# Three whole up blocks instead of five, another order at two places of the out product, and a weight sum moved from a transfer to VectorE, in a transformer block on one Trainium2 core

## The chip, the cores and the metric

One core of a Trainium2 chip. The time is the device time of one execution in microseconds (us), as the median of several runs. The engines are TensorE (PE in the profile), VectorE (DVE), ScalarE (ACT), GpSimd (POOL) and SyncE (SP, which only issues DMAs here). Every engine works through its own list of instructions in order; semaphores hold an instruction back until another engine or a transfer has counted far enough. A change below 0.2% (5.5 us) can't be told from none here.

## What is computed

One block with 512 tokens and a width of 2048, in fp32: a modulation from a vector `c`, attention over a sliding window beside a gated linear recurrence, an out product, and a feed-forward part with a short convolution.

```python
mod = jax.nn.silu(c) @ w_mod[l] + b_mod[l]
sh1, sc1, g1, sh2, sc2, g2 = jnp.split(mod[:, None, :], N_MOD, axis=-1)
...
merged = jax.nn.sigmoid(gate_a) * y_a + jax.nn.sigmoid(gate_b) * y_b
x = x + g1 * rms_norm(merged @ w_out[l], post_mix_norm[l])
h = rms_norm(x, pre_ffn_norm[l]) * (1.0 + sc2) + sh2
y = conv_ffn(h, w_ffn_up[l], ffn_conv_w[l], ffn_conv_b[l], w_ffn_down[l])
x = x + g2 * rms_norm(y, post_ffn_norm[l])
```

`conv_ffn` is `u = h @ w_up`, its halves `a` and `b` (5504 columns each), a causal convolution of three taps on `a`, `gelu(a) * b`, and the product with `w_down`.

## The kernel before

**fp32 by three products.** Each operand is split into a high half (the value rounded to the type that TensorE multiplies in one pass) and a low half (the rest). ScalarE casts the high half (`split_hi`), VectorE subtracts it (`split_lo`), and TensorE adds hi x hi, lo x hi and hi x lo (`three`). A piece of weights is 128x1024 (512 KB), loaded into a ring of four raw buffers by SyncE's queue and split into two buffer pairs.

**The stages** in order: the start with the modulation, the heads, the pairs (gates and branch products, giving `merged`), the out product (pieces P3 to P3+31, two row blocks of 128 each, four column groups of 512), the norms and the transposition of `h2`, the up product (43 blocks of 128 columns of `a` and of `b`), the down product, the last norm. Between the pairs and the out product `merged` is split as well, row block by row block, into `m_hi` (ScalarE) and `m_lo` (VectorE). In the out product VectorE also adds up `g2` from 64 pieces of 256 KB that GpSimd's queue loads (`g2_half`, L2036), two per piece; the last five pieces are kept and multiplied row group by row group, so that the norms can start. After the product of a row group, VectorE and ScalarE form the norm, GpSimd stores the row group, and VectorE then scales it in place.

**Whole and cut blocks.** The first WHOLE = 5 blocks of the up product are multiplied plainly: four pieces of 24 matmuls over 512 tokens, 96 matmuls. The other CUT = 38 blocks are 2x2 products (two halves of the rows of `h2`, a and b columns of the weights, two halves of the tokens), done with seven products instead of eight, from sums of weights and sums of halves of `h2`. A piece of a cut block is 8 matmuls over [hi | lo] and 8 over the high half alone. The four raw pieces of a block are X11, X21, X12, X22; even blocks have them in `raw`, odd ones in `raw_odd`. The weight sums are X21 + X22 (`w_sums[:, 0]`), that plus X11 (`w_sums[:, 1]`), X12 plus the latter, and X11 + X21. Of these, X21 + X22 is made by a second load of X21 into `w_sums` (`cut_load_s1`) and an adding transfer of GpSimd's queue (`s1_sum`), X11 + X21 by an adding transfer (`s3_sum`), the others by VectorE (`w_sum`). Before each adding transfer GpSimd runs a tiny instruction for order (`pool_turn`, L2417). The sums of halves of `h2` (`half_step`, `half_hi`, `half_lo`) are made by VectorE and ScalarE during the whole blocks. `raw_odd` shares memory with them, so the loads of the second cut block wait for the last of them.

The order of everything is written out by hand in each engine's function; there is no scheduler.

## Time and profile before

| | us |
|---|---|
| median of 3 runs (2767.45 to 2768.26) | 2767.5 |
| the profiled execution | 2769.19 |
| its span, first to last instruction | 2767.7 |
| TensorE busy | 2690.7 (97%) |
| VectorE busy | 1813.0 (66%) |
| ScalarE busy | 1077.1 (39%) |
| GpSimd busy | 231.2 (8%) |

The mean granted clock of TensorE is 0.99 of full speed. A row of a timeline gives the start from the beginning of the span, the duration, the engine, the line, the operation with output<-input, the number of instructions merged into the row, and in brackets how long the engine had stood idle and what released it. Instructions overlap at their ends: matmuls of 512 columns last 0.39 us each and start 0.227 apart, so work is counted from start to start.

### The profile page before, as it was taken

The numbers are of one execution on the slowest core, as the hardware profiler recorded it, in microseconds if no ns is written. First come the engines' busy times: TensorE is split into PE (matmuls) and PEld (weight loads), VectorE is DVE, ScalarE is ACT, GpSimd is POOL, SyncE is SP. The second block draws the span as 40 slices with busy tenths as digits, with TensorE's granted clock in tenths as the row PEclk, the third lists the DMA queues.
The fourth block names the chain that finished last, engine by engine and source line by source line (L and its number), as shares of the span: only waits on it lengthen the run. The fifth ranks groups of instructions, "written<-read, shape, count | busy, mean of one in ns | idle before, by whom it ended". The sixth has DMA issues, their size and how long they took to land.

```text
span 2767.7 us, 41356 instructions
## 1 busy us (share of the span) xinstructions
PE 2690.7 (97%) x14334; PEld 2258.3 (82%) x14334; DVE 1813.0 (66%) x2746; ACT 1077.1 (39%) x1466; POOL 231.2 (8%) x342
## 2 busy tenths in 40 slices
PE   5999999999999999999989999999999999999998
PEld 4788888888788888878778788888888888888886
DVE  6856666666665665545676688888888883334334
ACT  4354444445522222232243344444444442223223
POOL 0030000000000000002200122221212110000000
PEclk8999999999999999999999999999999999999999
DMA  9942232322377777646733888878787856522222
GB/s 361 325 111 84 84 85 84 85 84 80 92 214 219 219 214 219 190 135 209 249 122 115 197 205 198 207 192 211 193 212 191 211 145 221 203 99 96 95 99 106
DMA packets 504710, 460.91 MB, mean 167 GB/s; under 512 B 23419, under 2 KB 418962, under 8 KB 501920
## 3 DMA queue, kind: packets, MB, share of 16 engines
q1 hardware_dynamic: 469584, 360.75, 44.2%
q0 software_dynamic: 25120, 94.54, 12.9%
q10 hardware_dynamic: 9904, 4.26, 0.6%
q8 instruction: 64, 1.05, 0.2%
q14 instruction: 38, 0.31, 0.0%
HBM read 398.66 MB, written 20.99 MB: 152 GB/s over the span
## 4 chain that ended last, share of the span: by engine, by line
PE 92%; DVE 3%; DMA 2%; ACT 1%; issue 1%; SPq 1%; DVEq 0%; POOL 0%; POOLq 0%; ACTq 0%
PE acc_bank L650 15%; PE acc_bank L652 15%; PE acc_bank L651 15%; PE acc_bank L1071 7%; PE acc_bank L1075 3%; PE bank_ta L1071 3%; PE bank_tb L1071 2%; PE bank_pb L1071 2%; PE two_banks L1071 2%; PE two_banks L650 2%; PE two_banks L651 2%; PE two_banks L652 2%; PE bank_ta L1075 1%; PE bank_pb L650 1%; PE bank_pb L1075 1%; PE bank_tb L1075 1%
## 5 line engine op out<-in xcount | busy, mean ns | idle before, releaser
L626 DVE TENSOR_TENSOR w_lo<-raw,w_hi 128x1024 fp32r<-128x1024 f32 x305 | 373.3, 1224 | 692.5 <-ACT w_hi L620 692.5
L620 ACT CAST w_hi<-raw 128x1024 fp32r<-128x1024 f32 x305 | 320.2, 1050 | 884.9 <-PE acc_bank L652 422.4
L650 PE MATMUL acc_bank<-h_hi,w_hi 128*128 128x512 f32 x1124 | 447.3, 398 | 6.4 <-DVE h_lo L1670 6.4
L652 PE MATMUL acc_bank<-h_hi,w_lo 128*128 128x512 f32 x1124 | 439.1, 391 | 0.0
L651 PE MATMUL acc_bank<-h_lo,w_hi 128*128 128x512 f32 x1124 | 438.7, 390 | 0.0
L650 PEld LDWEIGHTS acc_bank<-h_hi,w_hi 128*128 128x128 f32 x1124 | 211.6, 188 | 50.4 <-issue 6.5
L652 PEld LDWEIGHTS acc_bank<-h_hi,w_lo 128*128 128x128 f32 x1124 | 211.5, 188 | 45.3
L651 PEld LDWEIGHTS acc_bank<-h_lo,w_hi 128*128 128x128 f32 x1124 | 211.8, 188 | 41.9
L1071 PE MATMUL acc_bank<-h_pair,s_hi 128*128 128x512 f32 x608 | 152.2, 392 | 0.0
L1656 DVE SCALAR_TENSOR_TENSOR acc<-raw,csil,acc 128x512 f32<-128x512 f32 x180 | 135.1, 750 | 10.1 <-DMA raw<-in_w_mod_dram 5.6
L1071 PEld LDWEIGHTS acc_bank<-h_pair,s_hi 128*128 128x128 f32 x608 | 109.4, 189 | 19.5
L650 PE MATMUL acc_bank<-o_hi,w_hi 128*128 128x512 f32 x256 | 101.0, 394 | 0.6 <-DVE o_lo L1981 0.3
L652 PE MATMUL acc_bank<-o_hi,w_lo 128*128 128x512 f32 x256 | 99.7, 390 | 0.0
L651 PE MATMUL acc_bank<-o_lo,w_hi 128*128 128x512 f32 x256 | 99.6, 389 | 0.0
L650 PE MATMUL acc_bank<-w_hi,a_hi 128*128 128x512 f32 x246 | 95.7, 389 | 0.0
L651 PE MATMUL acc_bank<-w_lo,a_hi 128*128 128x512 f32 x246 | 95.7, 389 | 0.0
L652 PE MATMUL acc_bank<-w_hi,a_lo 128*128 128x512 f32 x246 | 95.7, 389 | 0.0
L2417 POOL TENSOR_TENSOR st<-ones 128x1 f32<-128x1 f32 x76 | 65.6, 864 | 310.2 <-DMA raw<-in_w_ffn_up_dram 141.1
L2147 DVE TENSOR_TENSOR w_lo<-raw,w_hi 128x1024 fp32r<-128x1024 f32 x57 | 69.6, 1221 | 33.3 <-ACT w_hi L1488 33.3
L1488 ACT CAST w_hi<-sums 128x1024 fp32r<-128x1024 f32 x38 | 40.0, 1052 | 130.7 <-DMA sums<-raw_odd 66.0
L2147 DVE TENSOR_TENSOR w_lo<-raw_odd,w_hi 128x1024 fp32r<-128x1024 f32 x57 | 69.6, 1220 | 30.4 <-ACT w_hi L1488 30.4
L2386 POOL DMA_DIRECT2D gain_scratch<-small x1 | 0.6, 554 | 1046.8 <-ACT small L1405 1046.8
(556 smaller groups left out, 5887.5 us busy)
## 6 DMA issues: line engine op xcount, KB each, us to landing
raw<-in_w_in_dram SPq DMA_DIRECT2D x148, 512.0 KB, 4.0
raw<-in_w_mod_dram SPq DMA_DIRECT2D x96, 512.0 KB, 4.5
raw<-in_w_ffn_up_dram SPq DMA_DIRECT2D x96, 512.0 KB, 7.0
raw<-in_w_ffn_down_dram SPq DMA_DIRECT2D x86, 512.0 KB, 3.6
raw_odd<-in_w_ffn_up_dram SPq DMA_DIRECT2D x76, 512.0 KB, 7.5
sums<-in_w_ffn_up_dram SPq DMA_DIRECT2D x38, 512.0 KB, 4.5
mods_low<-in_w_mod_dram SPq DMA_DIRECT2D x32, 512.0 KB, 9.4
raw<-in_w_out_dram SPq DMA_DIRECT2D x32, 512.0 KB, 4.2
```

The lines of the kernel that those rows point to most:

```text
L620: act.copy(w_pair(g, gp)[0][:], raw[n % RAW][:]).then_inc(hi_ready, 1)
L626: dve.tensor_tensor(w_l[:], raw[n % RAW][:], w_h[:].bitcast(F32), ALU.subtract).then_inc(lo_ready, 1)
L650: pe.matmul(o, stat[0], mov[0], start=start, stop=False)
L651: pe.matmul(o, stat[0], mov[1], start=False, stop=False)
L652: return pe.matmul(o, stat[1], mov[0], start=False, stop=stop)
L1071: pe.matmul(CUT_FULL[p], wh[:, k, :], mov[:, k, :], start=k == 0, stop=False)
L1075: pe.matmul(CUT_BANKS[p], wl[:, k, :], mov[:, k, 0:H], start=False, stop=False)
L1488: act.copy(S_HI[S_PAIR[p]][:], cut_source(s, p)).then_inc(hi_ready, 1)
L1656: return STT(dst, w, cs, dst, ALU.mult, ALU.add).then_inc(mod_ops, 1)
L2147: TTe(S_LO[S_PAIR[p]][:], cut_source(s, p), S_HI[S_PAIR[p]][:].bitcast(F32), ALU.subtract).then_inc(lo_ready, 1)
L2386: pool.dma_start(g_scr[0:KT], small[0:KT, 0, 0:P]).then_inc(grow_stored, 16)
L2417: pool.tensor_tensor(st[:, 1:2], ones[:, 0:1], ones[:, 0:1], ALU.add).then_inc(pool_order, 1)
```

## The change

- WHOLE is 3 and CUT is 40.
- X21 + X22 is made by VectorE (`w_sum(s, it, 1)`), right before the first split of that block; the second load of X21 and its adding transfer go. `s3_sum` waits for VectorE's sum, since it overwrites X21.
- The halves of `h2` that the sums start from are kept by ScalarE during the transposition (`keep_y`, 16 copies), in place of three sums of high and low halves by VectorE afterwards; the remaining half steps stand in the two looped whole blocks.
- At the start of the out product VectorE's column operations and first weight split stand before the last product of the pairs, its last merge after two low halves of `merged`, and the third weight split after fourteen; TensorE starts with the eight matmuls of row block 0 that need only high halves.
- The 64 g2 additions go by `g2_done`: one or two per piece at first, then three, all done by piece 25, where they were two per piece to the end.

```diff
-WHOLE = 5
+WHOLE = 3
...
-            def cut_load_s1(s, it):
-
-                sp.dma_start(w_sums[:, 0, :].rearrange("p (k n) -> p k n", k=8), cut_cols(s, it, 0, 1)).then_inc(s1_landed, 16)
-
...
+                        if g == P3 and k == 0:
+                            pe.wait_ge(mh_ready, 1)
+                            for t4 in range(TT):
+                                for part in (wh, wl):
+                                    pe.matmul(OUT_BANKS[bank_set][t4], m_hi[:, 0, t4 * P:(t4 + 1) * P], part[:, 0, :],
+                                              start=part is wh, stop=False)
+                            pe.wait_ge(m_split, 1)
+                            for t4 in range(TT):
+                                pe.matmul(OUT_BANKS[bank_set][t4], m_lo[:, 0, t4 * P:(t4 + 1) * P], wh[:, 0, :], start=False, stop=False)
+                            continue
...
+            def keep_y(kb):
+
+                act.wait_ge(h2x, kb + 1)
+                if kb < 8:
+                    act.copy(RO[8]["y_top"][:, :, kb, :], small[:, kb % 4, :].rearrange("p (h t) -> p h t", h=2)).then_inc(hh_ready, 1)
+                else:
+                    act.copy(y_raw[22][:, kb - 8, :], small[:, kb % 4, H:T]).then_inc(hh_ready, 1)
...
-            weighed(3, KT // 2 - 1)
-            merge(1, KT // 2 - 1)
-
             dve.wait_ge(mod_taken, SUMS_LAST)
...
             split_lo(dve, P3, N3)
+            weighed(3, KT // 2 - 1)
             for kb in range(KT):
                 if kb == 2:
+                    merge(1, KT // 2 - 1)
                     split_lo(dve, P3 + 1, N3 + 1)
+                if kb == 14:
+                    split_lo(dve, P3 + 2, N3 + 2)
...
-            for i in range(2, 34):
-                if i < 32:
-                    split_lo(dve, P3 + i, N3 + i)
-                if i == 2:
-                    dve.wait_ge(multiplied, P3)
-                for half in range(2):
-                    g2_half(2 * (i - 2) + half)
+            def g2_done(i):
+                return min(max(0, i - 3, 3 * i - 12), 4 * KT)
+
+            dve.wait_ge(multiplied, P3)
+            for i in range(3, 32):
+                split_lo(dve, P3 + i, N3 + i)
+                for j in range(g2_done(i), g2_done(i + 1)):
+                    g2_half(j)
...
-                if n == 2:
-                    dve.wait_ge(s1_ready, 16 * (s + 1) + it * 32)
+                if n == 1:
+                    cut_landed(dve, s, it, X21)
+                    cut_landed(dve, s, it, X22)
+                    TTe(w_sums[:, 0, :], cut_raw(s, X21), cut_raw(s, X22), ALU.add).then_inc(s1_ready, 1)
+                elif n == 2:
+                    dve.wait_ge(s1_ready, s + 1 + it * 2)
...
                 else:
+                    w_sum(s + 1, it, 1)
                     cut_lo(s + 1, it, 0)
...
-            def s1_sum(s, it=0):
-
-                pool.wait_ge(s1_landed, 16 * (s + 1) + it * 32)
-                cut_landed(pool, s, it, X22)
-                pool_turn(2 * s + 1, it)
-                pool.dma_start(w_sums[:, 0, :], cut_raw(s, X22), accum_op=ALU.add).then_inc(s1_ready, 16)
...
                 cut_landed(pool, s, it, X21)
-                pool_turn(2 * s, it)
+                pool.wait_ge(s1_ready, s + 1 + it * 2)
+                pool_turn(s, it)
```

VectorE's list at the start of the out product, before the change. `small` and `merged` are the last products and merges of the pairs, `w_lo` the weight splits, `m_lo` the low halves of `merged`:

```order
L1987 TENSOR_TENSOR small<-small,acc_bank 128x512
L1991 TENSOR_TENSOR merged<-small 128x512
L2002 SCALAR_TENSOR_TENSOR a<-modc,vec 128x16
L2003 TENSOR_TENSOR gcol<-modc,vec 128x16
L626 TENSOR_TENSOR w_lo<-raw,w_hi 128x1024
L2010 TENSOR_TENSOR m_lo<-merged,m_hi 128x512 x2
L626 TENSOR_TENSOR w_lo<-raw,w_hi 128x1024
L2010 TENSOR_TENSOR m_lo<-merged,m_hi 128x512 x14
L626 TENSOR_TENSOR w_lo<-raw,w_hi 128x1024
```

The same place after the change:

```order
L2014 SCALAR_TENSOR_TENSOR a<-modc,vec 128x16
L2015 TENSOR_TENSOR gcol<-modc,vec 128x16
L616 TENSOR_TENSOR w_lo<-raw,w_hi 128x1024
L2002 TENSOR_TENSOR small<-small,acc_bank 128x512
L2025 TENSOR_TENSOR m_lo<-merged,m_hi 128x512 x2
L2006 TENSOR_TENSOR merged<-small 128x512
L616 TENSOR_TENSOR w_lo<-raw,w_hi 128x1024
L2025 TENSOR_TENSOR m_lo<-merged,m_hi 128x512 x12
L616 TENSOR_TENSOR w_lo<-raw,w_hi 128x1024
```

The column operations and the first weight split moved ahead of the last product, the merge behind two low halves, and the third weight split ahead of the last two.

VectorE's list at the change from one cut block to the next, in the second block, before the change. `sums` are the weight sums, `s_lo` and `w_lo` splits, `small` and `acc` sums of results:

```order
L2147 TENSOR_TENSOR s_lo<-raw_odd,s_hi 128x1024
L2147 TENSOR_TENSOR w_lo<-raw,w_hi 128x1024
L2182 TENSOR_TENSOR small<-acc_bank,small 128x256
L2154 TENSOR_TENSOR sums<-sums,raw 128x1024
L2172 TENSOR_TENSOR small<-acc_bank,small 128x256
L2147 TENSOR_TENSOR w_lo<-sums,w_hi 128x1024
```

The same place after the change:

```order
L2162 TENSOR_TENSOR s_lo<-raw_odd,s_hi 128x1024
L2170 TENSOR_TENSOR sums<-raw 128x1024
L2162 TENSOR_TENSOR w_lo<-raw,w_hi 128x1024
L2201 TENSOR_TENSOR small<-acc_bank,small 128x256
L2173 TENSOR_TENSOR sums<-sums,raw 128x1024
L2191 TENSOR_TENSOR small<-acc_bank,small 128x256
L2162 TENSOR_TENSOR w_lo<-sums,w_hi 128x1024
```

One row is new, the sum from two raw pieces (L2170); the others keep their order.

## Rows read from the trace of the kernel before

**Rows 1.** The page: the chain that ended last, by engine

```profile
PE 92%; DVE 3%; DMA 2%; ACT 1%; issue 1%; SPq 1%; DVEq 0%; POOL 0%; POOLq 0%; ACTq 0%
```

**Rows 2.** Busy us of PE, PEld, DVE, ACT, POOL in a stretch; clock, DMA

```profile
1640.00:1740.00 100.00, 100.00 (x573) 87.93 (x573) 87.76 (x135) 46.82 (x56) 21.77 (x27) 1.00 0.83 203
```

**Rows 3.** TensorE's timeline, two stages: start us, us, instruction, count [idle before <-releaser]

```profile
1499.87 0.39 PE L650 MATMUL acc_bank<-h_pair,w_hi 128*128 128x512 f32 x1
...
1500.55 0.39 PE L650 MATMUL acc_bank<-h_pair,w_hi 128*128 128x512 f32 x1
...
1916.35 2.00 PE L1071 MATMUL two_banks<-h_pair,w_hi 128*128 128x512 f32 x8
...
1935.91 2.00 PE L1071 MATMUL two_banks<-h_pair,w_hi 128*128 128x512 f32 x8
```

**Rows 4.** TensorE's timeline, the first two cut blocks

```profile
1535.23 1.98 PE L1071 MATMUL two_banks<-h_pair,w_hi 128*128 128x512 f32 x8
...
1542.19 1.10 PE L1075 MATMUL bank_ta<-t,w_lo 128*128 128x256 f32 x7 [1.41 <-DVE w_lo L2147]
...
1564.35 3.78 PE L1071 MATMUL bank_ta<-t,w_hi 128*128 128x512 f32 x8 [4.18 <-ACT w_hi L1488]
...
1572.78 2.00 PE L1071 MATMUL bank_pb<-h_pair,w_hi 128*128 128x512 f32 x8
```

**Rows 5.** ScalarE's timeline in the second cut block

```profile
1563.25 1.05 ACT L1488 CAST w_hi<-sums 128x1024 fp32r<-128x1024 f32 x1 [12.47 <-DMA sums<-raw_odd]
```

**Rows 6.** GpSimd's timeline in the second cut block

```profile
1553.51 0.86 POOL L2424 DMA_DIRECT2D sums<-raw_odd  x1
```

**Rows 7.** TensorE's timeline at the start of the out product

```profile
1221.48 0.47 PE L650 MATMUL acc_bank<-w_hi,m_hi 128*128 128x512 f32 x1 [1.55 <-DVE m_lo L2010]
...
1225.89 0.40 PE L650 MATMUL acc_bank<-w_hi,m_hi 128*128 128x512 f32 x1
```

**Rows 8.** VectorE's timeline at the start of the out product

```profile
1218.01 0.69 DVE L1987 TENSOR_TENSOR small<-small,acc_bank 128x512 f32<-128x512 f32 x1 [4.03 <-PE acc_bank L652]
...
1219.51 1.22 DVE L626 TENSOR_TENSOR w_lo<-raw,w_hi 128x1024 fp32r<-128x1024 f32 x1
1220.65 1.28 DVE L2010 TENSOR_TENSOR m_lo<-merged,m_hi 128x512 fp32r<-128x512 f32 x2
```

**Rows 9.** ScalarE's timeline at the start of the out product

```profile
1220.05 7.38 ACT L1403 CAST m_hi<-merged 128x512 fp32r<-128x512 f32 x14
```

**Rows 10.** TensorE's timeline in the last column group of the out product

```profile
1376.17 0.50 PE L650 MATMUL two_banks<-out_hi,m_hi 128*128 128x512 f32 x1 [1.70 <-DVE out_lo L626]
...
1379.40 0.50 PE L650 MATMUL two_banks<-w_hi,m_hi 128*128 128x512 f32 x1 [1.56 <-DVE w_lo L626]
```

**Rows 11.** VectorE's timeline in the last column group

```profile
1373.37 1.61 DVE L2036 SCALAR_TENSOR_TENSOR x_again<-y,csil,x_again 128x512 f32<-128x512 f32 x2 [0.61 <-DMA y<-in_w_mod_dram]
...
1376.61 1.60 DVE L2036 SCALAR_TENSOR_TENSOR x_again<-y,csil,x_again 128x512 f32<-128x512 f32 x2 [0.49 <-DMA y<-in_w_mod_dram]
1378.13 1.22 DVE L626 TENSOR_TENSOR w_lo<-raw,w_hi 128x1024 fp32r<-128x1024 f32 x1
```

**Rows 12.** VectorE's timeline after the out product

```profile
1401.01 1.28 DVE L2070 TENSOR_SCALAR y<-y,st 128x2048 f32<-128x2048 f32 x1 [3.16 <-DMA x_scratch<-y]
```

**Rows 13.** VectorE's timeline in a cut block of the loop

```profile
1928.73 1.22 DVE L2147 TENSOR_TENSOR s_lo<-raw_odd,s_hi 128x1024 fp32r<-128x1024 f32 x1
...
1940.34 1.23 DVE L2147 TENSOR_TENSOR w_lo<-raw,w_hi 128x1024 fp32r<-128x1024 f32 x1 [1.75 <-ACT w_hi L1488]
```

**Rows 14.** Adding transfers into the sums: count, KB each, median us to landing

```profile
sums<-raw POOLq DMA_DIRECT2D x19, 512.0 KB, 7.0
```

**Rows 15.** ScalarE's timeline in the same block

```profile
1941.69 1.05 ACT L1488 CAST w_hi<-raw 128x1024 fp32r<-128x1024 f32 x1 [0.86 <-PE bank_ta L1076]
```

**Rows 16.** GpSimd's timeline: one instruction, early and in the loop

```profile
1532.78 0.18 POOL L2417 TENSOR_TENSOR st<-ones 128x1 f32<-128x1 f32 x1 [11.45 <-DMA sums<-in_w_ffn_up_dram]
...
1923.93 0.99 POOL L2417 TENSOR_TENSOR st<-ones 128x1 f32<-128x1 f32 x1
```

More of the change, by code:

```diff
@@ L177, in block_kernel @@
             [(f"t{n}", [P, 8, T], F32R) for n in (1, 2, 3)]
-            + [(f"y{n}", [P, 8, H], F32) for n in (21, 11, 12, 22)],
+            + [("y21", [P, 8, H], F32), ("y_top", [P, 2, 8, H], F32), ("y22", [P, 8, H], F32)],
             [("t_home", [P, 6, 8, H], F32R), ("raw_odd", [P, 4, PIECE], F32), ("sums", [P, 2, PIECE], F32),
@@ L200, in block_kernel @@
         end_hi, end_lo, end_ah, end_al = (RO[10][n] for n in ("end_hi", "end_lo", "end_ah", "end_al"))
-        y_raw = {n: RO[8][f"y{n}"] for n in (11, 12, 21, 22)}
+        y_raw = {11: RO[8]["y_top"][:, 0], 12: RO[8]["y_top"][:, 1], 21: RO[8]["y21"][:], 22: RO[8]["y22"][:]}
         raw_odd, w_sums, gelu_out = RO[9]["raw_odd"], RO[9]["sums"], RO[9]["gelu_out"]
@@ L297, in block_kernel @@
         t_step = sem("t_step")
-        s1_landed, s1_ready, s3_ready = sem("s1_landed"), sem("s1_ready"), [sem(f"s3_ready{i}") for i in range(2)]
+        s1_ready, s3_ready = sem("s1_ready"), [sem(f"s3_ready{i}") for i in range(2)]
         sums_ready, mid_out, halves = sem("sums_ready"), sem("mid_out"), sem("halves")
@@ L1410, in square_out @@
                    accum_out=ssg[:, 4 * cg + t4:4 * cg + t4 + 1]).then_inc(y1_sq, 1)
-            for i in range(2, 32):
+            for i in range(3, 32):
                 split_hi(act, P3 + i, N3 + i)
@@ L1441, in _ @@
                     act.wait_ge(h2_ready, kb - 3)
+                    act.wait_ge(hh_ready, KT + kb - 3)
                 A_(small[:, kb % 4, :], TURN6[kb % 6], ACT.Identity, scale=a1[:, 1, kb:kb + 1],
                    bias=modc[:, MOD_SH2 + kb:MOD_SH2 + kb + 1]).then_inc(h2x, 1)
+                if kb >= 2:
+                    keep_y(kb - 2)
                 if kb == 5:
@@ L1446, in _ @@
                     split_hi(act, P4 + 3, N4 + 3)
+            for kb in range(KT - 2, KT):
+                keep_y(kb)
             def half_hi(n, dst):
-                act.wait_ge(t_step, 4 + n)
-                act.copy(dst, y_raw[(11, 12, 22, 21)[n - 1]][:]).then_inc(hh_ready, 1)
+                act.wait_ge(t_step, (3, 2, 4, 5)[n - 1])
+                act.copy(dst, y_raw[(12, 11, 22, 21)[n - 1]]).then_inc(hh_ready, 1)
             def gelu(it):
+                if it == 1:
+                    act.wait_ge(hh_ready, 2 * KT)
                 act.wait_ge(conv_step, it * 3)
@@ L1465, in _ @@
                         act.copy(acc[0:KT, 0:P], SC1[0:KT, 0:P]).then_inc(grow_ready, 1)
-                    if it == 3 and k < 3:
-                        half_hi(k + 1, RO[8][("t1", "t3", "t2")[k]][:, :, 0:H])
+                    if it == 2 and k < 3:
+                        half_hi(k + 1, RO[8][("t3", "t1", "t2")[k]][:, :, 0:H])
             def cut_hi(s, it, p):
@@ L1475, in cut_hi @@
                     if p == 1:
[L1476 removed]
+                        act.wait_ge(s1_ready, s + 1 + it * 2)
                     elif p == 4:
@@ L2016, in conv @@
                 dve.wait_ge(gelu_ready, it)
+                if isinstance(it, int) and it == 0:
+                    dve.wait_ge(hh_ready, 2 * KT)
                 TS(cv, a[:], j(tap_c[2]), j(convb_c), ALU.mult, ALU.add).then_inc(conv_step, 1)
@@ L2036, in g2_half @@
                 return STT(dst, g2_in[j % 4], csil[:, kt:kt + 1], dst, ALU.mult, ALU.add).then_inc(mod_ops, 1)
-            for i in range(2, 34):
-                if i < 32:
-                    split_lo(dve, P3 + i, N3 + i)
-                if i == 2:
-                    dve.wait_ge(multiplied, P3)
-                for half in range(2):
-                    g2_half(2 * (i - 2) + half)
+            def g2_done(i):
+                return min(max(0, i - 3, 3 * i - 12), 4 * KT)
+            dve.wait_ge(multiplied, P3)
+            for i in range(3, 32):
+                split_lo(dve, P3 + i, N3 + i)
+                for j in range(g2_done(i), g2_done(i + 1)):
+                    g2_half(j)
                 if i in (9, 17, 25):
@@ L2136, in _ @@
                         dve.wait_ge(multiplied, P4 + 4)
-                    if it < 3:
+                    if it == 1 or k == 0:
                         half_step(4 * (it - 1) + k)
-                    if it == 3 and k < 3:
-                        n = (1, 3, 2)[k]
-                        half_lo(k + 1, RO[8][f"t{n}"][:, :, 0:H], RO[8][f"t{n}"][:, :, H:T])
+                    else:
+                        n = (3, 1, 2)[k - 1]
+                        half_lo(k, RO[8][f"t{n}"][:, :, 0:H], RO[8][f"t{n}"][:, :, H:T])
             def cut_lo(s, it, p):
```

43 lines of the change are left out of this document (15 added, 28 removed).

## The prediction

> **What bounds the kernel now.** I read the page first, then the waits of TensorE in order of time, then the neighbours of each wait. The chain that ended last is 92% TensorE [rows 1]: only TensorE's own work and its pauses count. In the loop of cut blocks it is busy for 100 us out of 100 at full clock, VectorE for 87.8 [rows 2]. So the reader should look for TensorE work that goes, and for pauses outside that loop.
>
> The work: in a whole block three matmuls start within 0.68 us (1499.87 to 1500.55), and it has 96, so 21.76 us; a cut block takes 1935.91 - 1916.35 = 19.56 us, seven pieces of 2.794 us [rows 3].
>
> The pauses that the change touches are three. At the entry of the cut blocks, ten pieces take from 1535.23 to 1572.78, 37.55 us, where they need 10 x 2.794 = 27.94: 9.6 us are lost [rows 4]. In the second block TensorE stands 4.18 us, and the eight matmuls behind it then take 3.78 us where the same eight take 2.00 (the lower of its two clock levels, 1.2 for 2.4 GHz). What it waits for is ScalarE's cast of the sum X21 + X22, and that one had stood 12.47 us for the adding transfer [rows 5], issued at 1553.51 and landed at 1563.25, 9.7 us later [rows 6].
>
> At the start of the out product, the matmuls run from 1221.48, and the thirteenth starts at 1225.89 [rows 7]. The last piece before it ends at 1218.0: VectorE's product that waits for it starts at 1218.01 [rows 8]. From 1218.0 to 1225.9 TensorE does work worth 12 x 0.2267 = 2.7 us in 7.9: 5.2 us lost, of which 1.7 to the lower clock (1225.89 - 1221.48 = 4.4 us for 2.7 of work). VectorE has its merge, two column operations and a split of 1.22 us (from 1219.51) before the first low half, at 1220.65 [rows 8]. In the last column group TensorE pauses 1.70 and 1.56 us for a split [rows 10]; VectorE does that split late (1378.13) because it does g2 additions first, and stands 0.61 and 0.49 us in them for their own loads [rows 11].
>
> **The change part by part.** *Two whole blocks become cut ones.* 2 x (21.76 - 19.56) = 4.4 us off TensorE's path. The two also bring 2 blocks of VectorE work, which lies beside TensorE.
>
> *The sum X21 + X22 by VectorE.* A load of 512 KB and an adding transfer go; VectorE gets one addition of 128x1024 before its first split of the next block. The trace has the same form at 1.23 us (the split at 1940.34 reads two such operands and writes one [rows 13]), 1.14 from start to start. At the entry: the raw pieces of the first cut block are loaded during the last whole block, so VectorE can add them right after that block's last split, convolution and half matrix, before TensorE is done with it; the cast follows when its buffer is free, about 1535.3 (one matmul group past 1535.23), and TensorE wants it at 1535.23 + 2.79 = 1538.0. For the second block the four loads start when the last half matrix is split (estimate 1537.5), and the addition stands after the last split of the first block (estimate 1550, from the same place in the loop: 1928.73 is 7.2 us before 1935.91, and the second block would start at 1554.8). TensorE wants its cast at 1535.23 + 8 x 2.794 = 1557.6. Nothing of the 9.6 us is left by this count. I take all 9.6. The ends are 4 (rival one) and 9.6; below nothing is excluded, since the transfer that TensorE waited for 4.18 us isn't there any more.
>
> In the loop VectorE goes from 87.8% to (0.878 x 19.56 + 1.14) / 19.56 = 94%. The addition pushes what is queued behind it by 1.14 us: the next block's first two splits, the second sum, and the output sums. VectorE stands 1.75 us before the fourth split, waiting for ScalarE [rows 13], and takes it up there. Cost 0. If that cover were gone, it would cost 1.14 us a block at most, 46 us over 40 blocks, and only once the lead was used up that VectorE has here: it starts these splits 7.2 us before TensorE starts the block (1928.73 to 1935.91).
>
> A wait is added: GpSimd's other adding transfer (X21 += X11) overwrites X21, so it now comes after VectorE's addition, at about 1931.1 in the block shown, plus GpSimd's small ordering instruction, about 1.0 (its row is below), plus 7.0 from issue to landing [rows 14]: 1939.1. ScalarE casts it at 1941.69 [rows 15], and TensorE needs the cast at 1935.91 + 4 x 2.794 = 1947.1, so the data by 1946.0: 2.6 us ahead of ScalarE, 6.9 ahead of TensorE. Behind the transfer in GpSimd's queue stands only the store of an activation, whose slot is used again two blocks later. Cost 0, bounded by the 9.7 us of rows 6 as well, where 4.2 us of lead are left.
>
> GpSimd's small instruction takes 0.18 us early and 0.99 in the loop, where VectorE is busy [rows 16]. The Trainium skill (SBUF — State Buffer, "SBUF: two separate sides") says that a VectorE operation with two SBUF inputs and a GpSimd operation that reads SBUF exclude each other for a whole instruction. The trace agrees so far as these two rows go. By that rule the added operation can hold GpSimd up by one more such instruction, 1.2 us per block, and the transfer lands at 1940.3 instead of 1939.1: the sum stays, and rival four would decide 1.2 us earlier, for which I would give it 0.06 in place of the chance below.
>
> *The start of the out product.* The weight split stands before the last product of the pair stage, and TensorE's first eight matmuls need only the high half: they can start when that product is done, 1218.01 + 0.69 = 1218.7. The pause falls to 0.75 us and I take the clock as kept. The third weight split now stands behind 14 low halves: start of the first 1218.63, two, the merge, a split, twelve more at 0.61 each, so it ends at 1230.1, and TensorE wants it at 1218.75 + 96/2 x 0.2267 = 1229.6. That costs 0.45. ScalarE is no later: its casts are 0.53 us apart (7.38 for 14 [rows 9]). Gain 5.2 - 1.2 = 4.0; with the clock lost again 2.3.
>
> *The g2 additions* are done by piece 25, three per piece from the fifth. Then nothing stands between the last splits, and the pauses of 1.70 and 1.56 go: 3.3 us. What is late next is the last piece's own load, which the split frees one addition earlier than before. In pieces 5 to 25 VectorE does three additions of 0.8 (two take 1.61 [rows 11]) and a split of 1.14 in the 24 x 0.2267 = 5.44 us of a piece, beside TensorE. Everything after the out product starts 3.3 us earlier, but VectorE waits there 3.16 us for a store that GpSimd issues only after TensorE's g2 sum [rows 12]; that sum moves with TensorE, so I count the 3.3 once.
>
> *ScalarE's 16 copies in the turn of h2* (0.5 us each) lie in its waits for TensorE; they replace VectorE's first three sums of halves. Cost 0: TensorE gets its h2 rows several steps ahead. Of the half steps that were spread over three whole blocks, eight now stand in two, one to a piece; at 1.22 us for 1024 columns I estimate 2.4 for 2048, and with the split 3.6 of the 5.44 us of a piece. At the last piece the convolution comes on top (three passes, some 2.2), once, with the lead of a split behind it.
>
> Sum: 4.4 + 9.6 + 4.0 + 3.3 = 21.3 us. The profiled execution takes 2769.19 us (span 2767.7 and 1.5 around it), so 2747.9; the median of the runs, 2767.5, is 1.7 below it, so **2746.2 us**.
>
> **The rivals.** *One: the second cut block still stands.* The second adding transfer of that block now waits for VectorE's addition, about 1551.6, and is issued at 1552.5 in the busiest stretch of DMA; with the 9.7 us of rows 6 it lands at 1562.3, with its cast 1563.4, where TensorE wants it at 1535.23 + 11 x 2.794 = 1566.0. Only 2.6 us stand between. If it fails, a pause and the slow clock behind it come back, as in rows 4: about 5.5 of the 9.6 us, so 2751.7.
>
> *Two: the g2 loads hold VectorE.* When VectorE took them as fast as they came, two additions went in 1376.61 - 1373.37 = 3.24 us, 1.62 each [rows 11]; three need 4.9 of 5.44. A 1 MB load on the same queue comes in three times. Should each addition take 2.0, three and a split no longer fit, VectorE falls behind by up to 0.6 us a piece for 20 pieces, and after some 4 us of lead TensorE waits for up to 8: 2754.
>
> *Three: more comes.* VectorE no longer adds after the last piece, so its first row product starts sooner; if the 3.16 us of rows 12 go too, 2743.0. Against it: the store is behind the same TensorE sum.
>
> *Four, the other side: the adding transfer is late in every block.* If VectorE's addition and GpSimd's order bring it past 1946.0, TensorE waits in every one of 40 blocks. It decides when issue to landing passes 7.0 + 6.9 = 13.9 us, and the kernel is slower than before by over 0.2% from 27 us / 40 = 0.67 us per block, 14.6. At 1 us per block: 2746.2 + 40 = 2786. Against it: 9.7 is the longest seen in these rows, and a load and a transfer per block are gone from the DMA queues.
>
> **How the numbers follow.** Forecast 0.61, rival one 0.12, two 0.09, three 0.13, four 0.04; 0.01 is left for no effect. The range takes in one, two and three: 2742 to 2754. A difference below 0.2% (5.5 us) can't be told from none in this measurement. Faster 0.94, same 0.02, slower 0.04.
>
> **What would show it.** In the profile after: cut blocks 19.56 us apart, 40 of them; no wait of TensorE over 1 us in the first two; the first matmul of the out product under 1 us after the last before it, and the matmuls behind it 0.227 us apart; no wait in the last column group; VectorE at about 94% in the loop. Wrong it is if TensorE waits for the cast of X21 anywhere in the loop, if TensorE's clock falls at the out product, or if VectorE's waits for g2 loads reach TensorE.

## The result, and the profile after

The kernel after takes 2746.17 us (median of 4 runs, 2745.74 to 2747.52), the kernel before 2767.88 (4 runs, 2767.45 to 2769.34): ratio 0.9923, 95% interval [0.9911, 0.9935]. The forecast was 2746.2. The spans of the two profiled executions are 2746.0 and 2767.7.

The page of the kernel after: busy time by engine, and the shares of the chain that ended last.

```profile
PE 2680.0 (98%) x14366; PEld 2252.8 (82%) x14366; DVE 1867.1 (68%) x2819; ACT 1092.0 (40%) x1494; POOL 174.3 (6%) x270
...
PE 93%; DVE 2%; DMA 1%; ACT 1%; issue 1%; SPq 0%; DVEq 0%; POOL 0%; ACTq 0%; POOLq 0%
```

The bound is the same engine [rows 1], so the 21.7 us must be TensorE work or TensorE pauses. I cut both spans at three marks: VectorE's last product of the pair stage, TensorE's first row of the first up block, and the third piece of the last cut block.

| stretch, us | before | after | difference |
|---|---|---|---|
| up to the last pair product | 1218.01 | 1217.42 | -0.6 |
| from there to the first up row | 201.73 | 194.85 | -6.9 |
| up blocks, whole and cut | 855.8 | 841.6 | -14.1 |
| the rest | 492.2 | 492.1 | -0.1 |

The forecast was -7.3 for the second line and -14.0 for the third. Each column is one trace. The experiments below give the scatter: in six more traces that change nothing of the second stretch it is 194.4 to 195.1, in six that leave the up blocks alone the third is 841.3 to 841.7, and the mark of the first line lies between 1216.2 and 1218.9 in all of them, so the 0.6 there says nothing.

**The entry of the cut blocks.** TensorE's timeline at the first and second cut block (start, duration, line, operands, count).

```profile
1484.12 1.98 PE L1071 MATMUL two_banks<-h_pair,w_hi 128*128 128x512 f32 x8
...
1486.88 2.00 PE L1071 MATMUL bank_ta<-t,w_hi 128*128 128x512 f32 x8
...
1503.64 2.00 PE L1071 MATMUL two_banks<-h_pair,w_hi 128*128 128x512 f32 x8
...
1512.02 2.00 PE L1071 MATMUL bank_pb<-h_pair,w_hi 128*128 128x512 f32 x8
```

The ten pieces that took 37.55 us [rows 4] take 1512.02 - 1484.12 = 27.90, and a block 19.52 to 19.56. The wait of 4.18 us and the slow matmuls behind it are gone, as forecast. In the loop VectorE is busy for 93.23 of 100 us (87.76 in [rows 2], 94 forecast), TensorE for 100:

```profile
1640.00:1740.00 100.00, 93.23 (x141) 1.00 0.60 148
```

**The moved transfer.** One block of the loop in the kernel after: VectorE's new addition and its fourth split, then GpSimd's ordering instruction and adding transfer, ScalarE's cast of its result, and TensorE's matmuls that need it.

```profile
1908.22 1.22 DVE L2170 TENSOR_TENSOR sums<-raw 128x1024 f32<-128x1024 f32 x1
...
1918.69 1.23 DVE L2162 TENSOR_TENSOR w_lo<-raw,w_hi 128x1024 fp32r<-128x1024 f32 x1 [1.06 <-ACT w_hi L1503]
```

```profile
1909.61 1.02 POOL L2438 TENSOR_TENSOR st<-ones 128x1 f32<-128x1 f32 x1 [17.16 <-DVE sums L2170]
1910.57 0.86 POOL L2446 DMA_DIRECT2D raw<-raw  x1
```

```profile
1920.05 1.06 ACT L1503 CAST w_hi<-raw 128x1024 fp32r<-128x1024 f32 x1 [0.86 <-PE bank_ta L1076]
```

```profile
1925.44 2.00 PE L1071 MATMUL acc_bank<-t,w_hi 128*128 128x512 f32 x8
```

The fourth split's wait is 1.06 us instead of 1.75 [rows 13]: part of the addition was taken up there. This transfer now lands 4.6 us after its issue, at 1915.2. In the kernel before it took 6.7 us (median); the 7.0 of [rows 14], with which the prediction reckoned, is the other adding transfer's. At the same time the mean share of the DMA engines in 100 us of the loop fell from 0.83 [rows 2] to 0.60. ScalarE waits only for a buffer of TensorE. TensorE needs the data by 1925.44 - 1.05 = 1924.4, so the lead is 9.2 us; 6.9 was forecast, with the slower landing.

**The out product.** TensorE's start, its two later pauses, and the g2 sum of one-column matmuls at its end.

```profile
1218.23 0.47 PE L944 MATMUL acc_bank<-w_hi,m_hi 128*128 128x512 f32 x1 [0.74 <-DVE small L2002]
...
1229.57 0.50 PE L640 MATMUL acc_bank<-w_hi,m_hi 128*128 128x512 f32 x1 [0.19 <-DVE w_lo L616]
...
1241.19 0.50 PE L640 MATMUL acc_bank<-w_hi,m_hi 128*128 128x512 f32 x1 [0.45 <-DVE w_lo L616]
...
1380.07 3.63 PE L977 MATMUL acc_bank<-ones,x_again 128*128 128x1 f32 x32
```

Of [rows 7] a pause of 0.74 is left; the third split is late by 0.19 (0.45 forecast); the two pauses of the last column group [rows 10] are gone. The 0.45 at 1241.19 was not forecast. VectorE's timeline there, and behind the product, with GpSimd's two issues that the second row waits for:

```profile
1239.52 0.49 DVE L2051 TENSOR_SCALAR x_again<-y,csil 128x512 f32<-128x512 f32 x1 [7.66 <-DMA y<-in_w_mod_dram]
...
1393.53 1.29 DVE L2088 TENSOR_SCALAR y<-y,st 128x2048 f32<-128x2048 f32 x1 [8.43 <-DMA x_scratch<-y]
```

```profile
1383.99 0.53 POOL L2422 DMA_DIRECT2D x_again<-in_x_dram  x1 [38.96 <-PE acc_bank L977]
1384.51 0.54 POOL L2425 DMA_DIRECT2D x_scratch<-y  x1
```

The first g2 load holds VectorE for 7.66 us and, through the next split, TensorE for 0.45: a g2 load that reaches TensorE, which the prediction had named as a sign of being wrong. GpSimd issued it at 1231.10 (1230.71 in the kernel before), and VectorE could start on it at 1239.52 (1236.34 before, in a row below); why it took longer to land no run isolates. Four of the eight traces with the same code up to here don't have this pause.

The wait for the store, 3.16 us in [rows 12], has grown to 8.43: VectorE comes to it sooner, and the store still stands behind TensorE's g2 sum. What was late next, then, is this store.

### The profile page after: what moved, and what is told of

It is laid out like the page before. It is cut to its first block, busy times and chain, and to the rows that moved or that the text cites. A ratio compares the mean times of both kernels' runs of the same rounds, so it can differ in the third digit from the quotient of the medians.

```text
span 2746.0 us, 41393 instructions
## 1 busy us (share of the span) xinstructions
PE 2680.0 (98%) x14366; PEld 2252.8 (82%) x14366; DVE 1867.1 (68%) x2819; ACT 1092.0 (40%) x1494; POOL 174.3 (6%) x270
## 4 chain that ended last, share of the span: by engine, by line
PE 93%; DVE 2%; DMA 1%; ACT 1%; issue 1%; SPq 0%; DVEq 0%; POOL 0%; ACTq 0%; POOLq 0%
PE acc_bank L640 15%; PE acc_bank L642 15%; PE acc_bank L641 15%; PE acc_bank L1071 8%; PE acc_bank L1075 4%; PE bank_pb L1071 3%; PE bank_tb L1071 3%; PE bank_ta L1071 3%; PE two_banks L1071 3%; PE two_banks L640 2%; PE two_banks L641 2%; PE two_banks L642 2%; PE bank_ta L1075 1%; PE two_banks L1075 1%; PE bank_pb L1075 1%; PE bank_tb L1075 1%
## 5 line engine op out<-in xcount | busy, mean ns | idle before, releaser
L616 DVE TENSOR_TENSOR w_lo<-raw,w_hi 128x1024 fp32r<-128x1024 f32 x297 | 363.4, 1224 | 652.9 <-ACT w_hi L610 652.9
L610 ACT CAST w_hi<-raw 128x1024 fp32r<-128x1024 f32 x297 | 311.8, 1050 | 844.9 <-PE acc_bank L642 382.0
L1071 PE MATMUL acc_bank<-h_pair,s_hi 128*128 128x512 f32 x640 | 160.3, 392 | 0.0
L1071 PEld LDWEIGHTS acc_bank<-h_pair,s_hi 128*128 128x128 f32 x640 | 115.1, 189 | 20.6
L2162 DVE TENSOR_TENSOR w_lo<-raw,w_hi 128x1024 fp32r<-128x1024 f32 x60 | 73.2, 1221 | 21.9 <-ACT w_hi L1503 21.9
L1075 PEld LDWEIGHTS acc_bank<-h_pair,s_lo 128*128 128x128 f32 x560 | 77.7, 190 | 6.2
L2438 POOL TENSOR_TENSOR st<-ones 128x1 f32<-128x1 f32 x40 | 38.2, 955 | 676.1 <-DVE sums L2170 676.1
```

The lines of the kernel that those rows point to most:

```text
L610: act.copy(w_pair(g, gp)[0][:], raw[n % RAW][:]).then_inc(hi_ready, 1)
L616: dve.tensor_tensor(w_l[:], raw[n % RAW][:], w_h[:].bitcast(F32), ALU.subtract).then_inc(lo_ready, 1)
L1071: pe.matmul(CUT_FULL[p], wh[:, k, :], mov[:, k, :], start=k == 0, stop=False)
L1075: pe.matmul(CUT_BANKS[p], wl[:, k, :], mov[:, k, 0:H], start=False, stop=False)
L2162: TTe(S_LO[S_PAIR[p]][:], cut_source(s, p), S_HI[S_PAIR[p]][:].bitcast(F32), ALU.subtract).then_inc(lo_ready, 1)
L2438: pool.tensor_tensor(st[:, 1:2], ones[:, 0:1], ones[:, 0:1], ALU.add).then_inc(pool_order, 1)
```

## The experiments

All compute the whole result. Differences are against the kernel after, which was not run again beside them; the kernel before was, and took 2766.99 to 2767.62 us. Where medians are a few us apart, the stretches of the table above, taken from each trace, tell more than the medians.

**1. Five whole blocks.**

```diff
-WHOLE = 3
+WHOLE = 5
...
```

VectorE's half steps stay in the first two looped whole blocks.

> The kernel after with five whole blocks again instead of three (the 16 copies of the turn of h2 stay with ScalarE; nothing else is put back). My theory: a block costs TensorE 21.76 us whole and 19.56 us cut, and nothing else hangs on the number: 4.4 us longer than the kernel after, so about 2750.6. Rival (the two blocks were dear for more than TensorE's work, through what VectorE and the loads have to do beside them, or the entry of the cut blocks is only free because it comes early): clearly more than 4.4, 8 us or so. Rival (VectorE gains air): less than 3.

Measured: 2750.45 us (ratio to before 0.9941 [0.9927, 0.9955]), 4.3 over the kernel after; the up blocks take 846.0 us against 841.6. The price of a whole block is TensorE's work, 2.2 us, and nothing else that shows. Against the kernel before, which has as many whole blocks, the up blocks are 9.8 us shorter (855.8 to 846.0); that is the sum by VectorE and the 16 copies by ScalarE (with the three sums of halves that they replace) together.

**2. The sum X21 + X22 by a load and an adding transfer again.**

```diff
-                    TTe(w_sums[:, 0, :], cut_raw(s, X21), cut_raw(s, X22), ALU.add).then_inc(s1_ready, 1)
...
+                pool.dma_start(w_sums[:, 0, :], cut_raw(s, X22), accum_op=ALU.add).then_inc(s1_ready, 16)
```

> The kernel after with the sum X21 + X22 made again by a load of X21 and an adding transfer of GpSimd, in all cut blocks; three whole blocks stay. My theory: the loop stays at 19.56 us a block (TensorE is the bound with either), and the entry of the cut blocks stands again for the cast of the sum: 9.6 us longer (7 to 10). Rival (the 9.6 us were a matter of the load at the last whole blocks, and with three whole blocks they come out otherwise): under 4 or over 12. Rival (the sum by VectorE helps in the loop too): over 0.1 us per block more, 14 us or longer.

Measured: 2753.34 us (0.9952 [0.9938, 0.9965]), 7.2 over; the up blocks 849.3 against 841.6, so 7.7. TensorE waits in the first cut block now, and its clock falls behind the waits (eight matmuls in 2.81 us, then 3.22, instead of 2.00):

```profile
1491.50 2.81 PE L1081 MATMUL bank_ta<-t,w_hi 128*128 128x512 f32 x8 [2.94 <-ACT w_hi L1513]
1495.03 1.86 PE L1085 MATMUL bank_ta<-t,w_lo 128*128 128x256 f32 x7 [0.71 <-DVE w_lo L2172]
...
1496.90 3.22 PE L1081 MATMUL bank_tb<-t,s_hi 128*128 128x512 f32 x8
```

In the loop nothing is lost (TensorE at 100 of 100 us, VectorE at 87.86): the gain of VectorE's addition is at the entry alone. It is 7.7 here, where the kernel before lost 9.6; there two more whole blocks and three sums of halves by VectorE stood ahead of the entry, and no run tells which of these makes the difference. What the removed load and transfer did to their neighbour does show. The transfer X21 += X11 in this kernel, and then in the kernel after (count, size, median us to landing):

```profile
raw<-raw POOLq DMA_DIRECT2D x20, 512.0 KB, 6.9
```

```profile
raw<-raw POOLq DMA_DIRECT2D x20, 512.0 KB, 4.6
```

**3 to 6. The two seams of the out product.** The old start, with the g2 additions of after:

```diff
-            weighed(3, KT // 2 - 1)
...
+            weighed(3, KT // 2 - 1)
+            merge(1, KT // 2 - 1)
```

> The kernel after with the start of the out product as it was: the weight split behind the merge, TensorE takes the first tiles part by part, ScalarE's and VectorE's halves in the old order. My theory: the pause of 5.2 us comes back against 1.2 now, so 4.0 us longer (to 4.5, as the trace of after shows the third split late by 0.19 instead of 0.45), with TensorE's clock falling again behind the pause. Rival (the pause was covered by one later on that now takes its place: VectorE's low halves and g2 additions follow closely): under 2 us.

The old g2 order, with the start of after:

```diff
-            for i in range(3, 32):
-                split_lo(dve, P3 + i, N3 + i)
-                for j in range(g2_done(i), g2_done(i + 1)):
-                    g2_half(j)
+            for i in range(2, 34):
+                if 3 <= i < 32:
+                    split_lo(dve, P3 + i, N3 + i)
+                for half in range(2):
+                    g2_half(2 * (i - 2) + half)
```

> The kernel after with the g2 additions two per piece over all pieces of the out product, as they were. My theory as predicted: the two pauses of 1.70 and 1.56 us in the last column group come back, 3.3 us longer; the pause of 0.45 us at 1241.19 in the trace of after, in which VectorE was held 7.66 us by the first load of y, goes (2.8 in sum). Rival (given back later): behind the out product VectorE waits 8.43 us for a store in after and 3.16 in before, so a part of the gain was lost there; then this kernel is only 0 to 1 us longer.

Only TensorE's eight high-half matmuls first undone:

```diff
-                        if g == P3 and k == 0:
-                            pe.wait_ge(mh_ready, 1)
...
-                            continue
```

> The kernel after with one thing put back: at the start of the out product TensorE takes the first tiles part by part (high, high, low for each token tile) and not all eight high-half matmuls first. My theory: what removed the pause is the weight split that stands before the last product of the pair stage; with it both halves are there early, and the low half of the middle rows comes 0.6 us after the high one, so TensorE waits for it after two matmuls and not after eight: 0.2 to 1.0 us longer. Rival (the order of the matmuls is what gives the 4 us): 3 us or more.

The old g2 order with the first four g2 loads issued by GpSimd ahead of its wait for the gain's tile:

```diff
+            for j in range(4):
+                g2_load(j)
             pool.wait_ge(grow_ready, 1)
...
```

> The kernel after with the g2 additions two per piece as they were, but the first four g2 loads issued some 10 us earlier. With the old order alone the time was 11 to 12 us longer than after, by the traces 4.1 for a pause at the fourth piece (VectorE held 6.66 us by the first g2 load ahead of that piece's split), about 3 for the clock behind it, 3.1 for the last column group. My theory (that pause is the first load's, whose place in GpSimd's queue is behind a wait for ScalarE): only the last column group is left, 3.1 us longer than after. Rival (the old order is too slow at that place whatever the loads do, as VectorE's two additions stand before the split): 8 us or more.

Measured, with the stretch from the last pair product to the first up row:

| | median, us | ratio to before | stretch, us |
|---|---|---|---|
| before (old start, old g2) | 2767.88 | | 201.73 |
| old start, new g2 | 2748.76 | 0.9935 [0.9921, 0.9949] | 197.74 |
| new start, old g2 | 2758.28 | 0.9968 [0.9956, 0.9980] | 205.42 |
| new start, old g2, early loads | 2751.04 | 0.9941 [0.9927, 0.9954] | 197.99 |
| new start, new g2, matmuls part by part | 2747.70 | 0.9929 [0.9915, 0.9942] | 195.75 |
| after (new start, new g2) | 2746.17 | 0.9923 [0.9911, 0.9935] | 194.85 |

Read as a square: the new g2 order alone gives 4.0, both give 6.9, and the new start alone makes the stretch 3.7 us longer. (The kernel before differs in more than these two, but its pauses behind the out product, 1.98 and 5.95 us, are those of the run with the old start, 2.03 and 5.95, so it can stand in this corner.)

Going back to the old start costs 2.9 in the stretch and 2.6 in the median, where 4.0 was expected. TensorE's thirteenth matmul starts 7.9 us behind the mark again and not 3.6, but the pauses of 0.19 and 0.45 are then not there; what is left of the difference is within the scatter.

The expectation for the old g2 order, 2.8 to 3.3, missed by far: 10.6 us in the stretch, 12 in the median. TensorE's and VectorE's timelines of the new start with the old g2 order say why; the last fence gives the granted clock (third number from the end) of 1240 to 1262:

```profile
1240.39 0.79 PE L640 MATMUL acc_bank<-w_hi,m_hi 128*128 128x512 f32 x1 [4.57 <-DVE w_lo L616]
...
1379.79 0.50 PE L640 MATMUL two_banks<-out_hi,m_hi 128*128 128x512 f32 x1 [1.37 <-DVE out_lo L616]
...
1382.98 0.50 PE L640 MATMUL two_banks<-w_hi,m_hi 128*128 128x512 f32 x1 [1.53 <-DVE w_lo L616]
```

```profile
1237.85 0.48 DVE L2051 TENSOR_SCALAR x_again<-y,csil 128x512 f32<-128x512 f32 x1 [6.66 <-DMA y<-in_w_mod_dram]
...
1239.12 1.22 DVE L616 TENSOR_TENSOR w_lo<-raw,w_hi 128x1024 fp32r<-128x1024 f32 x1
```

```profile
1240.00:1262.00 22.00, 21.61 (x84) 0.86 0.64 214
```

GpSimd issues the first g2 load at about 1231 whatever TensorE does, because it stands in the queue behind a tile of ScalarE. In the old order VectorE waits for it ahead of the fourth piece's split. It did so in the kernel before as well (VectorE's timeline there):

```profile
1236.34 0.48 DVE L2034 TENSOR_SCALAR x_again<-y,csil 128x512 f32<-128x512 f32 x1 [3.71 <-DMA y<-in_w_mod_dram]
```

There TensorE was some 4 us later and did not feel it; started earlier, it stands 4.57 us, and at the lower clock level behind that it loses 0.14 x 22 = 3.1 more. The last column group adds 3.1. With 4.1 for the pause (4.57 less the 0.45 of after) these make 10.3 of the 10.6. In the order of after, one more split stands ahead of the first addition, and 0.45 is left. The run with early loads puts it to the test: expected +3.1 in the stretch, measured 197.99 - 194.85 = 3.14 (4.9 in the median), and behind the start the pauses of the last group are the only ones over 0.2 us:

```profile
1370.53 0.50 PE L640 MATMUL two_banks<-out_hi,m_hi 128*128 128x512 f32 x1 [1.45 <-DVE out_lo L616]
...
1373.64 0.50 PE L640 MATMUL two_banks<-w_hi,m_hi 128*128 128x512 f32 x1 [1.46 <-DVE w_lo L616]
```

The order of TensorE's first matmuls is worth 0.9 in the stretch, little more than its scatter: a first pause of 1.47 and one of 1.31 at the g2 load, instead of 0.74, 0.19 and 0.45. The other 2.0 of the 2.9 go to the places of the weight splits and the merge, which no run takes apart.

**7 and 8. The store behind the out product.** TensorE's g2 sum two token tiles earlier:

```diff
-                if t4 == 2:
+                if t4 == 0:
```

> The kernel after with TensorE's sum of g2 at the first token tile of its place and not at the third. What it is for: in the trace of after VectorE waits 8.43 us behind the out product for a store that GpSimd issues only behind that sum, and the g2 additions have long been done by then. My theory: the store is issued some 3 to 3.6 us earlier and the pauses of 2.14 and 5.95 us of TensorE behind the out product shrink by as much: 3.1 us shorter than after, 2743. Rival (the store waits for something else, a load in front of it in the queue): no change, within 0.5 us. Rival (TensorE's sum is itself held up at its new place): longer by up to 1 us.

The same with the four g2 loads issued early:

> The kernel after with two edits: TensorE's sum of g2 at the first token tile, and the first four g2 loads issued by GpSimd ahead of its wait for the small tile of the gain (1228.57 in the trace of after), so some 10 us earlier. My theory: the sum gives 2.2 to 2.9 us, and the loads take VectorE's wait of 7.66 us and the pause of 0.45 (0 to 0.5) away: 2742.9 to 2743.6. Rival (four more loads at the start of the out product slow the weight loads there): longer than with the sum alone, 2745 or more.

Measured: 2744.72 us (0.9921 [0.9907, 0.9934]) and 2746.24 (0.9921 [0.9907, 0.9934]); stretches 192.61 and 194.19 against 194.85. The store's wait is gone, since GpSimd comes to the load in front of it 14.6 us earlier (first kernel):

```profile
1369.36 0.54 POOL L2422 DMA_DIRECT2D x_again<-in_x_dram  x1 [25.55 <-PE acc_bank L977]
...
1382.67 0.54 POOL L2425 DMA_DIRECT2D x_scratch<-y  x1 [12.78 <-DVE y L2082]
```

By the trace this is 2.2 us better than the kernel after (3.1 was expected); by the medians the two can't be told apart. The early loads bring nothing on top, against the expectation of 2742.9 to 2743.6: with and without them TensorE's sum starts 148.3 us after the last pair product, so they gain nothing ahead of it, and the 1.6 us that this stretch is longer lie behind it. Part of the gain was lost at TensorE's sum itself (first kernel):

```profile
1365.24 3.82 PE L977 MATMUL acc_bank<-ones,x_again 128*128 128x1 f32 x32
1368.92 0.77 PE L640 MATMUL two_banks<-w_hi,m_hi 128*128 128x512 f32 x1
1369.49 0.63 PE L641 MATMUL two_banks<-w_lo,m_hi 128*128 128x512 f32 x1
```

TensorE counts as busy in the 32 matmuls of one column, but the ones behind start 0.43 us apart (lower clock level): seven of them, 1.5 us lost; in the kernel with early loads eleven, 2.3 us. In the kernel after they went on at 0.227 apart, yet with the same code in this stage (the addition twice, below) ten were slow (2.1 us). There the wait for the store hid it: its stretch is 195.13.

**9 and 10. VectorE's addition carried out twice, and three times.**

```diff
+                    TTe(w_sums[:, 0, :], cut_raw(s, X21), cut_raw(s, X22), ALU.add).then_inc(again, 1)
+                    dve.wait_ge(again, 1 * s + 1 + it * 2)
                     TTe(w_sums[:, 0, :], cut_raw(s, X21), cut_raw(s, X22), ALU.add).then_inc(s1_ready, 1)
```

> The kernel after with VectorE's addition X21 + X22 carried out twice in each cut block. VectorE has 19.56 x (1 - 0.932) = 1.3 us to spare per block, and the second addition with its wait costs 1.2 to 1.3. My theory (the spare time of VectorE is all that hides the addition, and it has a lead): the block stays at 19.56 us within 0.05, the kernel within 2 us of after, VectorE at 99%. Rival (an addition ahead of the next block's splits delays TensorE at once, since the splits are on its path): 1.2 us per block, some 48 us longer.

> The kernel after with VectorE's addition X21 + X22 carried out three times in each cut block: 18.24 + 2 x 1.25 = 20.7 us of VectorE's work in a block that TensorE does in 19.56. My theory: VectorE becomes the bound, a block takes 20.7 to 20.9, so 40 blocks cost 46 to 54 us more: 2793 to 2800. Rival (VectorE's share counts waits for ports and memory as work, so that it can be pressed together): under 20 us more. Rival (the splits' delay hits TensorE in full): 2.4 us per block, 96 us more.

Measured: 2747.87 us (0.9928 [0.9914, 0.9941]) and 2787.10 (1.0069 [1.0054, 1.0084]). VectorE's busy time in 100 us of the loop, with two and with three:

```profile
1640.00:1740.00 100.00, 98.92 (x146) 1.00 0.61 149
```

```profile
1640.00:1740.00 100.00, 99.66 (x144) 1.00 0.58 144
```

With two, 39 blocks take the same 762.6 us as in the kernel after; with three 796.1, 0.86 us per block. VectorE's addition starts 6.0 us ahead of TensorE's block in the kernel after, 4.8 ahead with two, and level with it with three. TensorE then waits once a block, at full clock:

```profile
1914.99 1.10 PE L1075 MATMUL two_banks<-h_pair,w_lo 128*128 128x256 f32 x7 [0.48 <-DVE w_lo L2162]
```

So the cover was real, and it ends where VectorE's share reaches 100%: one addition costs nothing, a second nothing, the third makes the kernel slower than before. The forecast of 20.7 us a block was 0.3 too high (20.4), which I can't split further. Another 5.7 us of the 40 are lost behind the loop, 3.6 of them in one pause of TensorE (0.6 in the kernel after). The profile puts it down to issue, but `down` waits there for VectorE's low half of an activation (`al_ready`), and the rows of the two engines fit:

```profile
2303.92 0.69 DVE L2282 TENSOR_TENSOR a_lo<-act,a_hi 128x512 fp32r<-128x512 f32 x1 [1.39 <-ACT a_hi L1560]
```

```profile
2304.71 0.77 PE L640 MATMUL two_banks<-w_hi,a_hi 128*128 128x512 f32 x1 [3.60 <-issue]
```

The low half is done at 2304.61 and TensorE starts 0.10 us later; in the kernel after it is done at 2266.87 and TensorE starts at 2266.98. VectorE has no lead left when the loop ends, and TensorE pays for it there.

**11 and 12. The adding transfer held back.** By a wait for VectorE's third, and then its fourth split of the same block:

```diff
+                pool.wait_ge(lo_ready, cut_piece(s, 2) + 1 + it * 14)
```

```diff
+                pool.wait_ge(lo_ready, cut_piece(s, 3) + 1 + it * 14)
```

> The kernel after with GpSimd's adding transfer (X21 += X11) held back in each cut block until VectorE's third split of that block: in the trace of after that split ends at 1915.6 in the block starting 1914.26, so the transfer is issued at 1916.7 and not 1910.57, and lands 4.6 us later at 1921.3; TensorE needs the data by 1924.4 (piece five at 1925.44, less ScalarE's cast). My theory (the lead is 9.2 us, and 6.1 of it can go): the kernel within 2 us of after. Rival (the transfer is tighter than that, by ScalarE's order or VectorE's queue behind the cast): 1 us per block or more, over 40 us longer.

> The same, held back until the fourth split of the block, which ends at 1919.8: issued 1920.9, landed 1925.5, cast 1926.5 where TensorE wants it at 1925.44. My theory (the fourth rival of the prediction, as a mechanism): TensorE waits 1.1 us in every block, and the wait comes again each time, since the split itself follows TensorE; 40 to 60 us longer than after, slower than before, with a wait of TensorE for ScalarE's cast once per block. Rival (something else has room, as the transfer gets faster alone in the queue): under 10 us.

Measured: 2757.10 us (0.9968 [0.9955, 0.9981]) and 2917.94 (1.0548 [1.0531, 1.0564]). First the wait for the third split: TensorE's one long wait of the stage, and GpSimd in the loop.

```profile
1499.06 3.78 PE L1071 MATMUL acc_bank<-t,w_hi 128*128 128x512 f32 x8 [4.59 <-ACT w_hi L1503]
```

```profile
1924.86 0.19 POOL L2438 TENSOR_TENSOR st<-ones 128x1 f32<-128x1 f32 x1 [17.64 <-DVE s_lo L2162]
1925.29 0.87 POOL L2447 DMA_DIRECT2D raw<-raw  x1 [0.24 <-issue]
```

In the loop TensorE loses nothing, its blocks stay 19.55 us apart: the block starts at 1920.29 and the transfer 5.0 us later, where in the kernel after it came 3.7 us ahead (1910.57, block 1914.26). That is 8.7 us later and not the 6.1 expected, since the third split itself has moved. VectorE pays instead: it waits for the late cast too, and its addition comes 4.6 us ahead of TensorE's block in the first half of the loop and 3.1 at its end, where it was 6.0 in the kernel after. The expected total was wrong, by the entry: there the transfer took 9.2 us to land and not 4.6, and TensorE lost 4.59 us and the clock behind, 7.1 in all. The other 3.5 are lost where the loop ends, 3.2 of them in the same pause as in experiment 10, again 0.10 us behind VectorE's low half (done at 2276.44):

```profile
2275.75 0.69 DVE L2278 TENSOR_TENSOR a_lo<-act,a_hi 128x512 fp32r<-128x512 f32 x1 [1.39 <-ACT a_hi L1560]
```

```profile
2276.54 0.47 PE L640 MATMUL two_banks<-w_hi,a_hi 128*128 128x512 f32 x1 [3.20 <-issue]
```

With the fourth split, TensorE and GpSimd in the loop:

```profile
1926.78 2.65 PE L1071 MATMUL acc_bank<-t,w_hi 128*128 128x512 f32 x8 [2.40 <-ACT w_hi L1503]
```

```profile
1919.35 1.62 POOL L2438 TENSOR_TENSOR st<-ones 128x1 f32<-128x1 f32 x1 [20.75 <-DVE w_lo L2162]
1920.91 0.86 POOL L2447 DMA_DIRECT2D raw<-raw  x1
```

The block starts at 1913.05, the transfer 7.86 later, which is 11.55 us later than in the kernel after. TensorE would have gone on at 1921.43 + 2.79 = 1924.22 and starts at 1926.78, 2.56 late, so the lead was 11.55 - 2.56 = 9.0 us: what the trace of after said (9.2). The price per block is 162.6 / 39 = 4.2 us and not the 1.1 expected. In the block shown it is 2.56 of standing and 1.6 of lower clock behind it; 29 of the 40 blocks have this pause, the others take turns between some 0.8 and 4 us. The standing is longer than expected because the split ended 0.5 us later in its block and GpSimd's small instruction took 1.62 us: the transfer was issued 7.86 us into the block, where the expectation had 6.6.

## Why the prediction was right

*Two whole blocks become cut ones, 4.4:* right (4.3 by experiment 1).

*The sum by VectorE, 9.6:* right for this change, 27.90 us for ten pieces of 27.94. As a price of this edit alone it is 7.7 with three whole blocks (experiment 2); the count had not asked where the wait would sit without the other edits, and no run puts the copies or the half steps back by themselves.

*Its cost in the loop, 0:* right, and for the reason given (experiment 9). I had bounded it by VectorE's lead; what decides is VectorE's share, 98.9% still free, three additions not.

*The moved transfer, 0, with 6.9 us of lead:* right; the lead is 9.0 to 9.2, for the transfer lands in 4.6 us now that a load and a transfer of each block are gone, and in 6.9 with them (experiment 2). The sum used 7.0, a landing time of before, which the change itself improved.

*The start, 4.0, and the g2 additions, 3.3:* the sum, 7.3, came out at 6.9, but these are not two terms. Alone the start costs 3.7 us, alone the g2 order gives 4.0. The prediction worked each out against the trace of before, where TensorE's late start covered the wait for the first g2 load (VectorE stood for it in the trace of before too, and nobody waited). It was right in the sum by luck in part: because both were made at once, and because the new g2 order also puts one more split ahead of that load, of which the prediction said nothing.

*ScalarE's 16 copies and the half steps, 0:* right. From the first up row to the first cut block it is 71.85 us with three whole blocks and 115.49 with five in the kernel before, which is 2 x 21.8 apart, a whole block's own 21.76.

*Rivals:* one did not come (no wait in the first two cut blocks). Two, that the pace of the g2 loads holds VectorE piece after piece, did not come either; the one 0.45 us is the first load's, by its place in GpSimd's queue. Three did not: the store's wait grew from 3.16 to 8.43, and the argument against it, that the store stands behind TensorE's sum, was the right one. Four, the slower side, is real as a mechanism (experiment 12), 9 us away; its price of 1 us per block left out the clock.

## What to carry to other kernels

Two edits at one engine's queue can each be priced from the trace of before and still not add: ask of each what the other's delay was hiding, above all a load whose issue time does not move when the engine that wants it starts earlier. A TensorE pause of 2.6 and one of 4.6 us cost some 60% as much again in clock behind them, so a wait that repeats per block is priced with both. And an engine beside the critical one could be filled to 99% here at no cost (experiment 9). But look at both ends of a loop, not only inside: experiment 11 lost nothing in the loop and 10.6 us in all, 7.1 at the first block, where the transfer took 9.2 us to land, and 3.5 behind the last, where VectorE's used-up lead was wanted.

## What the runs showed of the hardware

GpSimd's ordering instruction, one element per partition, takes 0.19 us or 1.02 or 1.62 in these kernels. In the kernel after it runs from 1909.61 and ends at 1910.6, where VectorE's split with two SBUF operands (1909.36, 1.22 us) ends; in experiment 12 from 1919.35 to 1920.97, over the rest of two such operations of VectorE (1919.10 and 1919.70 to 1920.92); in experiment 11, with an operation that reads a bank beside it, 0.19. These are the usual values: 34 of 40 at 0.93 or 1.02 in the kernel after, 32 of 40 at 1.62 or 1.63 in experiment 12, 37 of 40 at 0.18 or 0.19 in experiment 11. By these rows it waits for the whole VectorE operation, and back to back for two.

TensorE's clock can fall behind 32 matmuls of one column (3.6 to 4.8 us) in which the profile shows it busy. Of the seven traces with the same code up to there it did in three (experiments 1, 9 and 10; in 9 the granted clock is 0.59 from 1384 to 1390) and not in four (the kernel after, experiments 2, 11 and 12; in the kernel after it is 1.00 from 1383.5 to 1388). What decides it stays open.

An adding transfer of 512 KB in SBUF landed after 9.7 us [rows 6], 7.0 [rows 14], 4.6 in the loop of after, and 9.2 at the entry in experiment 11. That a load and a second adding transfer per block make 6.9 out of 4.6 is shown by experiment 2; what makes the 9 us at the entry is not isolated.
